# Kernel study: key weights and cache loaded already turned, a stream's value product set one head later, an output quarter per tile, on one Trainium2 core

## What is computed

```python
def expand_kv(ckv, krope, w_uk, w_uv):
    k_nope = (ckv @ w_uk).reshape(B, S, H_B, NOPE)
    ...
    v = (ckv @ w_uv).reshape(B, S, H_B, V_B)
def one(args):
    s = jnp.einsum('bqhd,bshd->bhqs', qi, k).astype(jnp.float32) * scale
    s = jnp.where(k_chunk[None, :] <= q_chunk[:, None], s, -jnp.inf)
    p = jax.nn.softmax(s, axis=-1).astype(v.dtype)
    return jnp.einsum('bhqs,bshd->bqhd', p, v)
...
o = mla_attend(q, k, v, q_offset).reshape(B, T, VD_B) * jax.nn.silu(gate)
return x + rmsnorm(o @ w_out, norm_post), S
```

## Time and profile before

| | us |
|---|---|
| median of 3 runs (lowest, highest) | 751.51 (749.87, 752.97) |
| profiled execution, its own time | 748.36 |
| span in its trace | 746.6 |
| PE busy | 668.5 (90%) |
| DVE busy | 444.0 (59%) |
| ACT busy | 294.9 (39%) |
| POOL busy | 178.8 (24%) |
| mean granted TensorE clock | 0.95 |

### The profile page before, as it was taken

One profiled execution on the slowest core, in us unless ns is written; L12 is line 12 of the kernel. 1 busy time (PEld: TensorE's weight loads), 2 busy tenths in 40 slices (PEclk: granted clock), 3 DMA queues, 4 the chain that ended last, 5 costly groups with the idle time before them and its releaser, 6 DMA issues.

```text
span 746.6 us, 12627 instructions
## 1 busy us (share of the span) xinstructions
PE 668.5 (90%) x4954; PEld 632.7 (85%) x4954; DVE 444.0 (59%) x651; ACT 294.9 (39%) x564; POOL 178.8 (24%) x179
## 2 busy tenths in 40 slices
PE   2796897999999977998899999989989999978995
PEld 1666896999999967997899989988878787878995
DVE  4416328467558566226765767536778878785324
ACT  5264423233234133235422422644465565544221
POOL 4500104306117034116342410320202122110004
PEclk9788998999999989999899999898999999999999
DMA  9302303613425254213123410433221111207103
GB/s 305 91 0 58 101 13 104 185 56 112 125 64 169 57 176 142 57 58 137 68 79 88 134 36 6 138 105 100 61 60 60 45 31 58 64 2 278 34 1 141
DMA packets 73261, 67.19 MB, mean 90 GB/s; under 512 B 13154, under 2 KB 69730, under 8 KB 73075
## 3 DMA queue, kind: packets, MB, share of 16 engines
q1 hardware_dynamic: 73202, 66.39, 28.8%
HBM read 55.60 MB, written 10.78 MB: 89 GB/s over the span
## 4 chain that ended last, share of the span: by engine, by line
PE 61%; DVE 22%; ACT 8%; issue 5%; POOL 2%; DMA 0%; SPq 0%; DVEq 0%; ACTq 0%; POOLq 0%
PE bank L1265 19%; PE bank L1266 19%; PE bank L1267 19%; DVE slab_lo L979 4%; DVE pT_lo L979 2%; ACT prob L937 1%; DVE oT_lo L979 1%; DVE hat_lo L979 1%; PE bank L1305 1%; DVE sT_lo L979 1%; ACT slab_hi L767 1%; DVE stat L1241 1%; DVE kN_lo L979 1%; DVE stat L1215 1%; PE bank L1457 1%
## 5 line engine op out<-in xcount | busy, mean ns | idle before, releaser
L1265 PE MATMUL bank<-slab_hi,hat_hi 128*128 128x256 f32 (+1 forms) x600 | 173.4, 289 | 15.1 <-DVE hat_lo L979 10.0
L1266 PE MATMUL bank<-slab_lo,hat_hi 128*128 128x256 f32 (+1 forms) x600 | 171.5, 286 | 0.0
L1267 PE MATMUL bank<-slab_hi,hat_lo 128*128 128x256 f32 (+1 forms) x600 | 171.2, 285 | 0.0
L1265 PEld LDWEIGHTS bank<-slab_hi,hat_hi 128*128 128x128 f32 x600 | 118.3, 197 | 17.6 <-DVE hat_lo L979 10.6
L1266 PEld LDWEIGHTS bank<-slab_lo,hat_hi 128*128 128x128 f32 x600 | 118.6, 198 | 0.0
L1267 PEld LDWEIGHTS bank<-slab_hi,hat_lo 128*128 128x128 f32 x600 | 118.4, 197 | 0.0
L979 DVE TENSOR_TENSOR slab_lo<-stage,slab_hi 128x1024 fp32r<-128x1024 f32 (+4 forms) x75 | 91.0, 1213 | 18.5 <-ACT slab_hi L767 16.1
L1265 PE MATMUL bank<-hat_hi,slab_hi 128*128 128x320 f32 (+1 forms) x272 | 86.0, 316 | 1.3 <-DVE slab_lo L979 0.9
L767 ACT ACTIVATE slab_hi<-stage 128x1024 fp32r<-128x1024 f32 (+4 forms) x75 | 74.5, 994 | 28.6 <-issue 14.5
L1266 PE MATMUL bank<-hat_lo,slab_hi 128*128 128x320 f32 (+1 forms) x272 | 85.0, 313 | 0.0
L1267 PE MATMUL bank<-hat_hi,slab_lo 128*128 128x320 f32 (+1 forms) x272 | 84.8, 312 | 0.0
(11 more groups left out here) (320 smaller groups left out, 1598.1 us busy)
## 6 DMA issues: line engine op xcount, KB each, us to landing
stage<-in_a_w_in_dram SPq DMA_DIRECT2D x24, 512.0 KB, 4.7
stage<-in_b_w_in_dram SPq DMA_DIRECT2D x10, 512.0 KB, 4.2
st_s<-in_state_gla_dram SPq DMA_DIRECT2D x4, 1024.0 KB, 6.5
out_dram<-st_s SPq DMA_DIRECT2D x4, 1024.0 KB, 5.2
stage<-in_a_w_out_dram SPq DMA_DIRECT2D x8, 512.0 KB, 4.6
craw<-in_cache_ckv_dram SPq DMA_DIRECT2D x8, 512.0 KB, 4.6
stage<-in_b_w_out_dram SPq DMA_DIRECT2D x8, 512.0 KB, 4.5
stage<-in_b_w_uq_dram SPq DMA_DIRECT2D x16, 192.0 KB, 2.7
```

Source lines behind the costliest of these rows:

```text
L1265: pe.matmul(out, a[0], b[0], start=first, stop=False)
L1266: pe.matmul(out, a[0], b[1], start=False, stop=False)
L1267: return pe.matmul(out, a[1], b[0], start=False, stop=last)
```

## The change

Three arrays are turned in `kernel()` before the launch and are inputs of their own: `ckvT` and `kropeT` (the cache) and `w_ukT` (the key weights). `wt` goes, and `qabs` reads the weights as loaded. `ct` and `cr` are no longer TensorE's: `ldc` loads the turned cache too (`sT_raw`, `sk_raw`, the rotary one twice), ACT copies the hi half and POOL subtracts it for the lo half. `sv` of a stream and `cs` of the next stand in the next head, behind `T`; `cx` comes a head later. `y A 0` waits tile by tile, and the pieces of `wo A 1` are split behind the turned tiles. `y B 0` stands ahead of `cx 7`. In the start of layer B, `qr 0` and `qr 1` come ahead of `gb 2 1`, `gb 1 0` behind `qr 4`, and the slabs are dealt out anew: `pre` 0 to 2 share one, `gb 0` takes that of `gb 1`. Memory placement changes with it (left out below).

```diff
+    def absorbed(h):
+        return ("b_w_uq", 0, KQ, h * (NOPE + ROPE), NOPE, "b_q_norm"), ("w_ukT", h, h + 1, 0, KL, None)
     out = {"glr": [[("a_w_in", 0, KD, 2 * HA * DK + 2 * HA * DV, RANK, "a_norm_pre")]]}
...
     uqr = [[("uq_rope", 0, KQ, h * ROPE, 4 * ROPE, "b_q_norm")] for h in (0, 4)]
-    pre = {("pre", p): [list(nope(2 * p + i)) for i in range(2)] for p in range(HB // 2)}
+    pre = {("pre", p): [list(absorbed(2 * p + i)) for i in range(2)] for p in range(HB // 2)}
     for name in (("gb", 3), ("gb", 2), "uqr", ("gb", 1), ("pre", 0), ("pre", 1), ("gb", 0), ("pre", 2), ("pre", 3)):
...
 SLAB_AT = {name: n % 2 for name, n in SLAB_NO.items()}
+SLAB_AT["pre", 1] = SLAB_AT["pre", 2] = SLAB_AT["pre", 0]
+SLAB_AT["gb", 0] = SLAB_AT["gb", 1]
 SLAB_AT["wo", "B", 1], SLAB_AT["wo", "B", 2], SLAB_AT["wo", "B", 3] = 2, SLAB_AT["uv"], SLAB_AT["wo", "B", 0]
...
                 out += [("gl", t), ("oT", t - EARLY_GATE)]
-            load(("wo", "A", 1))
             out += [("oT", t) for t in range(NT - EARLY_GATE, NT)]
+            load(("wo", "A", 1))
         else:
...
-        out += [("y", ph, 0), ("so",), ("soh",)]
+        out += [("y", ph, 0), ("cx", SB - 1), ("ldk",)]
+        load(("wo", ph, 1))
+        out += [("so",), ("soh",)]
         load(("wo", ph, 2))
...
     load("uqr")
-    out += [("gb", 2, 0)] + [("qT", t) for t in range(NT)] + [("gb", 2, 1)]
+    out += [("gb", 2, 0)] + [("qT", t) for t in range(NT)] + [("qr", 0), ("qr", 1), ("gb", 2, 1)]
     load(("gb", 1))
-    out += [("qr", 0), ("qr", 1), ("gb", 1, 0), ("qrT", 0), ("qr", 2), ("qrT", 1), ("qr", 3), ("qrT", 2), ("qr", 4)]
+    out += [("qrT", 0), ("qr", 2), ("qrT", 1), ("qr", 3), ("qrT", 2), ("qr", 4)]
     load(("pre", 0))
-    out += [("gb", 1, 1)]
-    out += [("qrT", 3), ("qns", 0), ("wt", 0)]
+    out += [("gb", 1, 0), ("qrT", 3), ("qns", 0), ("qrT", 4), ("qabs", 0)]
     load(("pre", 1))
+    out += [("gb", 1, 1), ("qns", 1)]
     load(("gb", 0))
-    out += [("qrT", 4), ("qabs", 0), ("qns", 1), ("wt", 1)]
+    out += [("qabs", 1)]
     load(("pre", 2))
-    out += [("gb", 0, 0), ("qabs", 1), ("qns", 2), ("wt", 2), ("ldc", 0), ("ldc", 1), ("gb", 0, 1)]
+    out += [("gb", 0, 0), ("qns", 2), ("qabs", 2)]
     load(("pre", 3))
+    out += [("gb", 0, 1), ("ldc", 0), ("ldc", 1)]
     load(("hd", 0))
-    out += [("qabs", 2), ("ct", 0), ("cr", 0), ("qns", 3), ("wt", 3)]
+    out += [("qns", 3), ("qn", 0), ("kh", 0), ("qabs", 3)]
     load(("hd", 1))
-    out += [("qn", 0), ("kh", 0), ("qabs", 3)]
+    out += [("ct", 0), ("cr", 0)]
...
         more = h + 1 < HB
-        out += [("S", h, 0), ("S", h, 1), ("N", h, 0), ("N", h, 1)]
-        if not more:
-            out += [("sv", h - 1)]
-        out += [("ss", h), ("cs", h)]
-        if h:
-            out += [("cx", h - 1)]
-        else:
+        out += [("S", h, 0), ("S", h, 1), ("N", h, 0), ("N", h, 1), ("ss", h)]
+        if h > 1:
+            out += [("cx", h - 2)]
+        elif h == 0:
             out += [("vh", 0)]
...
             out += [("qn", h + 1), ("kh", h + 1)]
-        out += [("T", h, 0), ("T", h, 1), ("st", h)]
+        out += [("T", h, 0), ("T", h, 1)]
+        if h:
+            out += [("sv", h - 1)]
+        out += [("cs", h), ("st", h)]
         if h + 2 < HB:
...
         out += [("O", h), ("Oh", h)]
-        if not more:
-            out += [("sv", h)]
-        if h + 2 < HB:
-            if h % 2:
-                out += [("vh", h // 2 + 1)]
-        if h + 2 < HB:
-            out += [("sv", h)]
+        if h + 2 < HB and h % 2:
+            out += [("vh", h // 2 + 1)]
+    out += [("cx", SB - 2), ("sv", SB - 1)]
     load("uv")
-    out += [("cx", SB - 1), ("ldk",)]
-    load(("wo", "B", 1))
...
-    "S": ("pe", "dve", "act"), "T": ("pe", "act", "dve"), "O": ("pe", "dve"), "ct": ("pe", "act", "dve"),
-    "cr": ("pe", "act", "dve"), "ss": ("pe", "dve", "act"), "cs": ("pool",), 
+    "S": ("pe", "dve", "act"), "T": ("pe", "act", "dve"), "O": ("pe", "dve"), "ct": ("act", "pool"),
+    "cr": ("act", "pool"), "ss": ("pe", "dve", "act"), "cs": ("pool",), 
...
 for _s in range(4):
-    USERS["gb", _s], USERS["pre", _s] = ("gb", _s, 1), ("wt", _s)
+    USERS["gb", _s], USERS["pre", _s] = ("gb", _s, 1), ("qabs", _s)
 for _h in range(HB):
...
-                        after(sp, "pe", "wt", 2)
+                        after(sp, "pe", "gb", 0, 1)
                     else:
                         after(sp, "pool", "cs", b - 2)
-                        after(sp, "pe", "cr", b - 2)
+                        after(sp, "pe", "ss", b - 2)
                     sp.dma_start(craw[b % 2][:, :, :], dram["cache_ckv"][b].rearrange("(s p) n -> p s n", p=P)).then_inc(cache_in[b % 2], 16)
-                    sp.dma_start(kraw[b % 2][:, :, :], dram["cache_krope"][b].rearrange("(s p) n -> p s n", p=P)).then_inc(cache_in[b % 2], 16)
+                    sp.dma_start(sT_raw[b % 2][:, :, :], dram["ckvT"][b]).then_inc(cache_in[b % 2], 16)
+                    for i in range(2):
+                        sp.dma_start(sk_raw[b % 2][i * ROPE:(i + 1) * ROPE, :], dram["kropeT"][b]).then_inc(cache_in[b % 2], 16)
                 elif kind == "oy":
...
                     b = step[1]
-                    pool.wait_ge(cache_in[b % 2], 32 * (b // 2 + 1))
+                    pool.wait_ge(cache_in[b % 2], 64 * (b // 2 + 1))
                     after(pool, "pe", *(("sv", b - 1) if b else ("gb", 0, 1)))
...
                     last = pool.tensor_tensor(cn[1][:, :, :], craw[b % 2][:, :, :], raw(cn[0][:, :, :]), SUB)
+                elif kind == "ct":
+                    after(pool, "act", *step)
+                    b = step[1]
+                    last = pool.tensor_tensor(sT_lo[b % 2][:, :, :], sT_raw[b % 2][:, :, :], raw(sT_hi[:, :, :]), SUB)
+                elif kind == "cr":
+                    after(pool, "act", *step)
+                    b = step[1]
+                    last = pool.tensor_tensor(skL[b % 2][:, :], sk_raw[b % 2][:, :], raw(skS[:, :]), SUB)
                 elif kind == "rx":
...
                     last = copy(qN_s[0][:, :], bank[:, 0, 0:2 * P])
-                elif kind == "wt":
-                    copy(wT[0][:, :], bank[:, 0, :])
-                    last = copy(wT[1][:, :], bank[:, 1, :])
                 elif kind == "kh":
...
                 elif kind == "ct":
-                    last = copy(sT[0][:, :, :], bank[:, :, :])
+                    b = step[1]
+                    act.wait_ge(cache_in[b % 2], 64 * (b // 2 + 1))
+                    if b:
+                        after(act, "pe", "ss", b - 1)
+                    else:
+                        after(act, "pe", "gb", 0, 1)
+                    last = copy(sT_hi[:, :, :], sT_raw[b % 2][:, :, :])
                 elif kind == "cr":
-                    copy(skS[0:ROPE, :], bank[0:ROPE, 0, :])
-                    last = copy(skS[ROPE:P, :], bank[0:ROPE, 0, :])
+                    last = copy(skS[:, :], sk_raw[step[1] % 2][:, :])
                 elif kind == "ss":
...
                     last = low(oT_lo[:, h, 0:SEQ], gateT[:, h, 0:SEQ], qS[:, h, :])
-                elif kind == "ct":
-                    last = low(sT[1][:, :, :], bank[:, :, :], sT[0][:, :, :])
-                elif kind == "cr":
-                    low(skL[0:ROPE, :], bank[0:ROPE, 0, :], skS[0:ROPE, :])
-                    last = low(skL[ROPE:P, :], bank[0:ROPE, 0, :], skS[0:ROPE, :])
                 elif kind == "ss":
...
                 for i, t in enumerate(tiles):
+                    if name[0] == "wo" and name[1] == "A":
+                        after(pe, "dve", "oT", t)
                     for k in range(kts):
...
                     ready(("wo", ph, s))
-                    after(pe, "dve", *(("oT", NP - 1 if kind == "y" else NP) if ph == "A" else ("Oh", HB - 2)))
+                    if ph == "B":
+                        after(pe, "dve", "Oh", HB - 2)
                     last = natural(row, ("wo", ph, s), range(NP) if kind == "y" else [NP], 256, KD, hat if ph == "A" else None)
...
                             last = mm3(bank[:, 0, i * P:(i + 1) * P], cut(w, A_, k), cut(qlT, A_, k, slice(SEQ, TOK)), k == 0, k == KQ - 1)
-                elif kind == "wt":
-                    for j, x in enumerate(weights(("pre", step[1]))):
-                        for i in range(2):
-                            for c in range(KC):
-                                at = i * PIECE + KQ * NOPE + c * NOPE
-                                last = pe.transpose(bank[:, j, (i * KC + c) * P:(i * KC + c + 1) * P], raw(x[:, at:at + NOPE]), ident)
                 elif kind == "kh":
...
-                    after(pe, "act", "wt", step[1])
                     after(pe, "dve", "qns", step[1])
...
                             j = (i * KC + c) * P
-                            last = mm3(bank[:, 0, j:j + P], cut(wT, A_, slice(j, j + P)), cut(qN_s, A_, slice(i * P, (i + 1) * P)), True, True)
+                            at = i * PIECE + KQ * NOPE + c * P
```

(19 more changed lines are left out.)

31 lines of the change are left out of this document (21 added, 10 removed).

## The result

The changed kernel takes 776.88 us (median of 4 runs, 774.99 to 778.41), the kernel before 750.92 beside it (749.87 to 752.97): a ratio of 1.034, 95% interval 1.031 to 1.038. That is 26 us slower. The forecast was 761 us, which is +9.3 by its sum, with a range of 743 to 774.

A forecast was written before the change was run, and what follows sets the result against it. TensorE, 90% busy, was taken as the bound, with new waits in the heads deciding. Terms -6.4 + 0 + 13.3 + 2.4 = +9.3 on 748.36 us profiled give 757.7; plus 3.15 for the median, 761 us, range 743 to 774.

The forecast's parts named there:

- Part 1: Gate product of stage A: y A 0 waits per tile and runs at full clock, gain 6.4 us.
- Part 2: 128 transposes leave TensorE, at 0.11 to 0.13 us each: 14 to 16 us of its time.
- Part 3: From gb 2 1 to the first ss: less work and slow clock, offset by new waits; 0, bounds -4 and +4.
- Part 4: Heads, first ss to y B 0: +1.3 us from waits plus 12 of half clock, +13.3; bounds +1 and +17.
- The chain: In the heads, ss waits for cn, weight piece, sT_lo and skL, starting 10.7 us after sv's end; +1.3 us.
- the last passage: Last stretch between ends of sv in the heads, without weight piece, qn or kh: 15.2 us.
- the tail: From the last passage to y B 0, with cn 7, sv 7 and the pieces of wo B 0: 7.5 us.
- Part 5: y B 0 ahead of cx 7: the wait ahead of so is 2.6 us instead of 0.1; +2.4, bounds 0 and 4.
- (a): Heads: the chain on POOL binds but the clock holds; 749 us, chance 0.20.
- (b): Heads: POOL and ACT keep ahead, TensorE stays the bound; -21 us for Part 4, 727 us, chance 0.13.
- (c): Heads: DVE and POOL block each other, 1.35 us in seven heads; +9.5, 770 us, chance 0.12.
- (d): The change does what it says, but half clock outlasts the estimate; up to 776 us, chance 0.07.

The follow-up runs named there:

- e17_kh_behind_t: Changed kernel, output quarters and start of layer B mended, heads reordered: qn, T, kh, cx, st, POOL's subtractions kept off DVE's normalizations, vh 0 before first ss; 724.76 us.
- e12_weights_alone: Kernel before with only the key weights loaded turned (wt and wT gone, qabs 1 and 2 directly behind their qns); 760.66 us, ratio 1.014.
- e11_filler: Changed kernel with 20 matmuls whose results are overwritten ahead of each wait at vh 1 to 3, ss 3 and ss 5; 761.60 us, ratio 1.015.
- e3_cx7_first: Changed kernel with cx 7, the load of the kept rows and the pieces of wo B 1 back ahead of y B 0; 770.37 us, ratio 1.029.
- e7_y_split: Changed kernel with y B 0 in two halves, cx 7 between them, kept rows and wo B 1 loaded behind sv 7; 767.83 us, ratio 1.023.
- e1_cs_behind: Changed kernel with POOL's cn of stream h moved behind sT_lo and skL of stream h+1; 756.79 us, ratio 1.011.
- e6_sv_back: Changed kernel with sv back at the end of its own head, cx in the next, POOL's order as in the change; 754.32 us, ratio 1.005.
- e16_cn_repeat: Kernel before with POOL's subtraction cn_lo done four times over in each head; 794.20 us, ratio 1.059.
- e5_head_early: Changed kernel with ct and cr of the next stream ahead of this stream's ss, and the weight piece ahead of S in odd heads; 758.00 us, ratio 1.008.

## Why the prediction was right or wrong

- **Part 1** (-6.4): measured -5.8 in the profile, -6.2 alone. y A 0 takes 11.44 at clock 1.00 without a gap, as said; y A 1 is slightly longer than in the earlier trace rows, 11.22 for 10.87; no run shows why.
- **Part 2**: TensorE is busy for 144.81 us in the heads before, and for 130.69, and 2.95 more of `vh` 0, in e17_kh_behind_t. That is 11 less for 84 transposes (12 in each of seven heads), 0.13 each; 0.11 to 0.13 was right, and 0.28 was not. But e12_weights_alone shows the step that Part 2 left out: what TensorE does in the place of the transposes. They had covered read-outs and freed a slab early.
- **Part 3** (0): measured +4.5. The work less (about 4.4 by busy time and clock, 4.9 forecast) and the waits more (14.1 in place of 5.9, +8.2; forecast +8.4) were right. The slow clock is the term that was mis-sized: it was to fall from 7 us to 4, but at a mean of 0.92 over 88.6 busy us it is again 7.
- **Part 4** (+13.3): measured +18.4. The chain was right to 0.3 us, and the last passage (15.2 forecast, 15.3 measured) and the tail (7.5, 7.6) too. The half clock was taken as 12 us and is 13.1. The chain's own term, +1.3, is +5.2: 1.9 of the difference lies ahead of the end of `sv` 0, where `O` 0 waits 1.9 us for `pT_lo`; there were twelve transposes in that place before, and the forecast did not have the wait. The other 2 are spread: at full clock, in e11_filler, the five passages take 23.3, 20.7, 22.9, 20.6 and 22.9 for the 22.7 and 20.3 of the forecast. (The prediction's 6.0 to the end of the two `S` is the sum of 0.7, 1.98 and 3.58, so 6.3; `ss` waits for the chain in any case.)
- **Part 5** (+2.4): measured +9.7. This is the step that failed most. The wait ahead of `so` was given 2.6 and is 3.4, but the sentence stopped there: the price of the half clock behind a wait, charged five times in Part 4, was not charged here. `so` ran its 48 matmuls in 9.87 us at 0.51, where e3_cx7_first has 5.47 at 1.00 (e7_y_split takes the same), and y B 1 lost 2 more.
- **The sum**: forecast +9.3, measured +26.8 by the stretches. The 17.5 between them are 7.3 of Part 5, 5.1 of Part 4, 4.5 of Part 3 and 0.6 of Part 1. Some 11 of them are half clock (6.4, 1.1 and 3.1 in Parts 5, 4 and 3). The 3.15 that the forecast added, because the median lay above the profiled time, was no property of the kernel: here the median lies 1.2 below it. So the profiled time is off by 20.4 and the median by only 15.9, and that is luck.
- **Rivals**: (a) fell, the clock did not hold. (b) fell for this change, but the gain that it priced is there: the heads of e17_kh_behind_t, whose order covers the waits, are 16 us shorter than before, for its 21. (c) was a real mechanism in the wrong place: in the changed kernel the chain holds TensorE so long that the subtractions seldom meet DVE's long instructions (from head 1 on the normalizations keep 0.68; `oT_lo` has 1.0 to 1.4 for 0.69 in heads 0 to 5), and it only came forward when the chain was cut. It was underpriced too, since the normalizations were left out. (d), the half clock beyond the estimate, up to 776, is the nearest to what happened, given 0.07; its size was right for about 11 of the 17.5.

Not settled: e1_cs_behind and e6_sv_back both stop near 155 us. In e6_sv_back 14.3 us are the wait ahead of `O`. In e1_cs_behind the waits are others (at `ss`, `vh` and `T`); that the blocked normalizations are the cause there is argued from its rows and from e16_cn_repeat, not shown by a kernel that differs in that alone. e17_kh_behind_t changes several places at once, so what each is worth is read from its waits, not from runs of their own.

## What to carry to other kernels

Work moved to an idle engine costs by its place in that engine's queue: ask what stands ahead of it, and what that waits for. Where a trace shows half clock behind TensorE's waits, charge each new wait twice, for itself and for the clock, wherever it stands; if it can't be removed, useless matmuls in it can pay. Before instructions are taken off the busiest engine, look which read-out they were covering and which buffer they freed, and whether a long POOL instruction will now fall on DVE's instructions that live in SBUF.

## What was not expected of the hardware

- Twenty useless matmuls per wait made the kernel 15 us faster.
- The half clock behind one wait of 3.4 us outlasts 48 matmuls without a gap (9.87 us at 0.51) and reaches into the 96 that follow (13.6 us from the first start to that of the step behind, 11.6 in e7_y_split).
- A POOL subtraction stops a DVE `TENSOR_SCALAR` whose operands are in SBUF, a small one as much as a large one: 1.52 us for one of 0.17 (128x2), 4.82 for a pair of 0.68. Beside the same subtractions a reciprocal (128x2) keeps its 0.17, and a `TENSOR_SCALAR` on one number per partition its 0.15.
- The work ahead of the first edit took up to 3.7 us more or less from profile to profile, at the same instructions. Up to `gb 2 0`, the same in the kernel after, e5_head_early and e7_y_split, the difference grows to 6.1.
